# The MLP of a decoder layer: up projection first by block products, then seven rounds of down products

## The reference, cut to what matters

```python
x = x + y                                   # y: the mixer, its last step is merged @ w_out
hm = rms_norm(x, norm_mlp)
x = x + jnp.square(jax.nn.relu(hm @ w_up)) @ w_down      # w_up 1024 x 4096, w_down 4096 x 1024
```

## Time and profile before

| | |
|---|---|
| median of 3 runs | 2209.72 us |
| span of the profiled execution (the page gives no other time of it) | 2207.2 us |
| MLP from its first matmul | 1475.5 to the end, 731.7 us |
| instructions | 33503 |
| HBM read, written | 135.62 MB, 34.89 MB |

### The profile page before, as it was taken

One profiled execution on the slowest core, in us unless ns is written; L12 is line 12 of the kernel. 1 busy time (PEld: TensorE's weight loads), 2 busy tenths in 40 slices (PEclk: granted clock), 3 DMA queues, 4 the chain that ended last, 5 costly groups with the idle time before them and its releaser, 6 DMA issues. The chain is left out here.

```text
span 2207.2 us, 33503 instructions
## 1 busy us (share of the span) xinstructions
PE 2188.0 (99%) x13547; PEld 2073.1 (94%) x13547; DVE 1112.9 (50%) x1749; ACT 658.2 (30%) x1158; POOL 1094.1 (50%) x1363
## 2 busy tenths in 40 slices
PE   8999999999999999999999999999999999999998
PEld 7999999999999999999999999889989889899897
DVE  8522221799764535534443566455364463553625
ACT  5444442333321111232222212133223232232332
POOL 4544444677343233222225564418475575754851
PEclk9999999999999999999999999999999999999999
DMA  5233332112121111222334555201211202102022
GB/s 180 95 99 100 107 104 69 49 49 69 53 89 51 48 42 52 58 60 80 90 121 141 174 186 169 97 16 43 77 30 49 70 8 77 58 20 77 20 67 81
DMA packets 172941, 172.31 MB, mean 78 GB/s; under 512 B 6722, under 2 KB 147334, under 8 KB 172779
## 3 DMA queue, kind: packets, MB, share of 16 engines
q1 hardware_dynamic: 169905, 159.87, 23.6%
q0 software_dynamic: 2304, 8.91, 1.1%
q10 hardware_dynamic: 578, 1.38, 0.2%
HBM read 135.62 MB, written 34.89 MB: 77 GB/s over the span
## 5 line engine op out<-in xcount | busy, mean ns | idle before, releaser
L967 PE MATMUL acc<-h_hi,w_hi 128*128 128x368 f32 (+2 forms) x2040 | 669.6, 328 | 0.5 <-issue 0.5
L969 PE MATMUL acc<-h_hi,w_lo 128*128 128x368 f32 (+2 forms) x2040 | 663.5, 325 | 0.0
L968 PE MATMUL acc<-h_lo,w_hi 128*128 128x368 f32 (+2 forms) x2040 | 662.8, 325 | 0.0
L1952 POOL TENSOR_TENSOR w_lo<-w_raw,w_hi 128x256 fp32r<-128x256 f32 x508 | 378.1, 774 | 470.1 <-ACT w_hi L1464 470.1
L967 PEld LDWEIGHTS acc<-h_hi,w_hi 128*128 128x128 f32 x2040 | 383.4, 188 | 5.5 <-issue 4.0
L968 PEld LDWEIGHTS acc<-h_lo,w_hi 128*128 128x128 f32 x2040 | 383.5, 188 | 0.2
L969 PEld LDWEIGHTS acc<-h_hi,w_lo 128*128 128x128 f32 x2040 | 383.3, 188 | 0.0
L1464 ACT ACTIVATE w_hi<-w_raw 128x1024 fp32r<-128x1024 f32 (+2 forms) x145 | 138.7, 957 | 358.9 <-PE acc L969 183.8
L2310 DVE TENSOR_TENSOR x<-pz,x 128x512 f32<-128x512 f32 x214 | 144.3, 688 | 90.9 <-PE pz L969 88.3
L1952 POOL TENSOR_TENSOR a_op<-a_raw,a_op 128x256 fp32r<-128x256 f32 x196 | 157.8, 843 | 24.6 <-DVE a_raw L2310 14.9
L2310 DVE TENSOR_TENSOR a_raw<-acc,a_raw 128x368 f32<-128x368 f32 (+1 forms) x112 | 44.8, 421 | 206.9 <-ACT a_raw L1827 118.7
(11 more groups left out here) (530 smaller groups left out, 4687.5 us busy)
## 6 DMA issues: line engine op xcount, KB each, us to landing
w_raw<-in_w_in SPq DMA_DIRECT2D x70, 512.0 KB, 4.3
w_raw<-in_w_up SPq DMA_DIRECT2D x32, 512.0 KB, 4.3
gate_values<-staging SPq DMA_DIRECT2D x29, 544.0 KB, 3.7
gsig<-gate_values SPq DMA_DIRECT2D x29, 544.0 KB, 3.7
w_raw<-in_w_down SPq DMA_DIRECT2D x18, 512.0 KB, 3.5
b_raw<-branch_outputs POOLq DMA_DIRECT2D x16, 544.0 KB, 5.5
w_raw<-in_w_branch SPq DMA_DIRECT2D x16, 512.0 KB, 4.8
g_raw<-in_w_in SPq DMA_DIRECT2D x14, 512.0 KB, 5.3
```

What stands on the lines that cost most here:

```text
L967: pe.matmul(out, lh, rh, start=first, stop=False, skip_group_check=more)
L968: pe.matmul(out, lh, rl, start=False, stop=False, skip_group_check=more)
L969: return pe.matmul(out, ll, rh, start=False, stop=last, skip_group_check=more)
L1952: return pool.tensor_tensor(out, x, y, op)
```

## The change

The whole up projection runs before the down projection. Its last four units are computed first and plainly; relu and square are both done by ACT into `staging` and the values are stored to DRAM. The other 28 units go in 14 pairs by seven block products, as at the gates, with sums `t_op` made anew from `h_hi` and `h_lo` by DVE. The residual is stored to DRAM for this (nine DMAs of 512 KB; t_raw takes its place) and is loaded back afterwards into the place of `h_hi`/`h_lo`. DVE adds and squares a pair's values, makes four sums of blocks for the down products, and SP stores these operands: 7 x 256 KB for a pair and 96 KB for the samples. Seven down rounds of seven stages follow without an up part between. u's operands are loaded, 512 KB a stage, into six places; ACT makes the high halves of the weights (`b_high`) and of u (`a_high`), GpSimd the low halves of both. In rounds 2 to 5 the stored values of the last four units are split too (`u_high`, `u_low`), for the end, which is computed as before. Cut to its core:

```diff
-L_UN, L_BN, L_GN, L_IT = 4, 4, 44, 8
+LAST, VP, NR = 4, 14, 7
+OPS_V = 7 * VP
+OPS_D = 7 * NR
+A_SLOTS = 6
+DVE_LO = []
+POOL_LO = [n for n in range(OPS_D) if n not in DVE_LO]
...
 TensorE
-            for i in range(END):
-                for s in range(4):
-                    up(i, s)
-                down(i)
-            for s in range(4):
-                up(END, s)
+            for e in range(LAST):
+                last_up(e)
+            up_pairs()          # as pairs(), weights w_up, 14 pairs
+            for i in range(NR):
+                down(i)
...
 down, TensorE: what a stage waits for
-                        pe.wait_ge(sem("op_lo"), OPS_G + 7 * i + st + 1)
-                        pe.wait_ge(sem("u_ready"), 16 * i + A_READY[st])
+                        pe.wait_ge(sem("op_lo"), OPS_G + OPS_V + n + 1)
+                        pe.wait_ge(*a_low_ready(n))
...
                         if st == 0:
-                            pe.wait_ge(sem("u_ready"), 16 * i + 11)
+                            pe.wait_ge(sem("packed"), i + 1)
...
 ScalarE
+            wide_hi(L_U + 1)
+            for e in range(LAST):
                 for g in range(3):
+                    last_square(e, g)
+                    if (e, g) in ((0, 2), (1, 0), (2, 0), (2, 1)):
+                        v_t_high(((0, 2), (1, 0), (2, 0), (2, 1)).index((e, g)))
+                    if g == 2 and e < 2:
+                        wide_hi(L_U + 2 + e)
...
+            for n in range(2, OPS_D):
+                a_high(n)
+                b_high(n)
+                if n % 7 == 1:
+                    pack_high(n // 7)
+                if n % 7 == 6 and 2 <= n // 7 < 6:
+                    u_high(n // 7 - 2)
...
 GpSimd
+            for e in range(1, LAST):
+                wide_lo(L_U + e)
+            for n in range(OPS_V):
+                v_low(n)
+            b_low(0)
+            a_low(0)
+            a_low(1)
+            for n in range(1, OPS_D):
+                b_low(n)
+                if n + 1 < OPS_D:
+                    a_low(n + 1)
+                if n % 7 == 6 and 2 <= n // 7 < 6:
+                    u_low(n // 7 - 2)
+            e_low(0)
+            e_low(2)
...
+            def a_low(n):
+                pool.wait_ge(hi_ready, L_U + LAST + n + 1)
+                for q in range(2):
+                    for c0 in (0, 256):
+                        c = slice(c0, c0 + 256)
+                        ins = tt(a_lo(n)[:, q, c], a_raw(n)[:, q, c], a_hi(n)[:, q, c].bitcast(F32), ALU.subtract)
+                ins.then_inc(w_ready, 1)
...
 VectorE
+            def v_t_sums():
...
+                dve.wait_ge(sem("b_stored"), 16 * H + 16 * (NT + 1))
+                dve.wait_ge(group_ready, L_G)
+                dve.wait_ge(sem("rows_to_lo"), 4 * (NT + 1))
+                ...                            # nine sums of 128x2176, in a chain
+                v_op_sums(0, (0, 1))
+                for n, t in ((2, 1), (1, 2), (3, 0), (4, 3)):
+                    dve.wait_ge(sem("t_hi"), 4 + n)
+                    tt(t_op[:, t, 1], t_raw[:, t, 1], t_op[:, t, 0].bitcast(F32), ALU.subtract) \
+                        .then_inc(sem("t_lo"), 1)
+                v_op_sums(0, (2,))
...
+            def up_pairs():
+                for j in range(VP):
+                    if j:
+                        v_op_sums(j, (2,))
+                        v_finish(j - 1)        # one square, four sums of 512, two small ones
+                    v_add(j, 1, "11", 0)
+                    v_square(j, "11", "g_dve", 6 * j + 2)
+                    v_op_sums(j, (3,))
+                    if j + 1 < VP:
+                        v_op_sums(j + 1, (0, 1))
+                    v_add(j, 4, "22", 4)
+                    v_square(j, "22", "g_dve", 6 * j + 4)
+                    v_add(j, 5, "21", 2)
+                    v_square(j, "21", "g_dve", 6 * j + 6)
...
+            v_t_sums()
+            up_pairs()
+            down_sums(0, 1)
+            v_finish(VP - 1)
+            dve.wait_ge(sem("g_done"), V_DONE + 2 * OPS_V - 4)
+            link(dve.memset(x1_s[TS:], 0.0))
+            pack_low(0)
...
 SyncE, between the pairs and the rounds
+            sp.wait_ge(sem("g_done"), V_DONE + 2 * OPS_V - 8)
+            op_load(0)
+            op_load(1)
+            sp.wait_ge(sem("op_lo"), OPS_G + OPS_V)
+            f1_load(0)
+            sp.wait_ge(sem("g_done"), V_DONE + 2 * OPS_V - 6)
+            op_load(2)
+            op_load(3)
...
+            for n in range(OPS_D):
+                i, st = n // 7, n % 7
+                if n + A_SLOTS < OPS_D:
+                    sp.wait_ge(group_ready, op_end(n))
+                    op_load(n + A_SLOTS)
+                if st == 3 and i + 1 < NR:
+                    sp.wait_ge(sem("op_sums"), SUMS_D + 8 * i + 8)
+                    sp.wait_ge(sem("op_lo"), OPS_G + OPS_V + 7 * i + 3)
+                    f0_load(i + 1)
+                    sp.wait_ge(sem("op_lo"), OPS_G + OPS_V + 7 * i + 6)
+                    f1_load(i + 1)
```

More of the change, by code:

```diff
@@ L514, in build @@
-        with ExitStack() as st:
[L515 to L522, removed]
+            sb(st, "pad_x", [P, 4832])
+            m_s = sb(st, "m_s", [P, KT, 2 * TS], F32R)
+            spill_o = sb(st, "spill_o", [P, 2, 512])[0:TS]
@@ L1395, in up @@
                         normed_in(g)
                     for k in range(KT):
-                        if first and g == 1 and k == 4:
+                        if e == 0 and g == 1 and k == 4:
                             turn_normed(NT)
-                        cols = slice(k % 4 * P, k % 4 * P + P)
-                        mm = product(acc[:, g, 0:c1 - c0], hi[k // 4][:, cols], lo[k // 4][:, cols],
-                                     h_hi[:, k, c0:c1], h_lo[:, k, c0:c1], k == 0, k == KT - 1)
+                        hi, lo = [w_tile(w, (L_U + e) % SLOTS, k, 0, P) for w in (w_hi, w_lo)]
@@ L1915, in _ @@
+            act.wait_ge(sem("l_added"), 32 * NR)
+            copy(spill_l, x1_s[TS:]).then_inc(sem("spilled"), 1)
             act.wait_ge(sem("folded"), 3)
@@ new lines, in v_t_sums, with made, h @@
+            def v_t_sums():
+                def made(out, x, y, op):
+                    tt(out, x, y, op).then_inc(sem("t_made"), 1)
+                def h(w, k, half):
+                    return w[:, 4 * k:4 * k + 4, half * HT:half * HT + HT].bitcast(F32)
+                dve.wait_ge(sem("b_stored"), 16 * H + 16 * (NT + 1))
+                dve.wait_ge(group_ready, L_G)
+                dve.wait_ge(sem("rows_to_lo"), 4 * (NT + 1))
+                t1, t2, t3, t4 = [t_raw[:, t, 1] for t in range(4)]
+                low = t_raw[:, 3, 0]
+                made(low, h(h_lo, 0, 1), h(h_lo, 1, 1), ALU.subtract)
+                made(t3, h(h_hi, 0, 1), h(h_hi, 1, 1), ALU.subtract)
+                v_t_made(2)
+                made(t3, t3, low, ALU.add)
+                v_t_made(3)
+                made(t2, h(h_hi, 0, 0), t3, ALU.subtract)
+                v_t_made(4)
+                made(t2, t2, h(h_lo, 0, 0), ALU.add)
+                v_t_made(5)
+                made(t1, h(h_hi, 1, 1), t2, ALU.subtract)
+                made(t4, h(h_hi, 1, 0), t2, ALU.subtract)
+                v_t_made(6)
+                made(t1, t1, h(h_lo, 1, 1), ALU.add)
+                v_t_made(7)
+                made(t4, t4, h(h_lo, 1, 0), ALU.add)
+                v_op_sums(0, (0, 1))
[4 more added lines that the diff above has]
+                v_op_sums(0, (2,))
@@ new lines, in v_square, with v_add @@
+            def v_square(j, corner, ready, count):
+                dve.wait_ge(sem(ready), (V_DVE if ready == "g_dve" else V_ACT) + count)
+                v = v_value(j, corner)
+                stt(v, v, 0.0, v, ALU.max, ALU.mult).then_inc(sem("v_squared"), 1)
+            def v_add(j, e, corner, copied):
+                for c in range(2):
+                    dve.wait_ge(sem("g_done"), V_DONE + 14 * j + 2 * e + c + 1)
+                    dve.wait_ge(sem("g_act"), V_ACT + 8 * j + copied + c + 1)
+                    v = v_value(j, corner, c)
+                    tt(v, v_bank(j, e, c), v, ALU.add).then_inc(sem("g_dve"), 1)
```

858 lines of the change are left out of this document (505 added, 353 removed).

## The result

The changed kernel takes 2221.3 us, the median of 4 runs (2220.2 to 2222.5), against 2209.8 beside it: ratio 1.0053, 95% interval 1.0039 to 1.0067. It is slower by 0.5%; I had forecast 2199 and called that side 0.14. The profiled execution has a span of 2218.4 us. First the page, part 1, to be held against the earlier trace rows.

The account below looks back on a forecast made before the run. TensorE, 99% busy, was taken as the bound. Profiled: 2207.2 - 35.8 (pairs) + 8.5 (start) + 2 (clock) + 5 (seam) + 10 (down rounds) = 2196.9 us, so 2199 timed; forecast range 2184 to 2205.

Parts of the forecast that it names:

- Seven down rounds: Rounds without an up part between: GpSimd's work about level with TensorE's 42.38 us a round, costing 10 us.
- rival A: Down rounds: GpSimd is the bound, from 0.757 us a subtraction on; 2230 us, slower than before; chance 0.12.
- Start: Start of the up part: GpSimd's subtractions slowed beside DVE's t_op instructions make TensorE wait, 8.5 us.
- Clock: After the start's wait and the next waits, TensorE runs some matmuls at a lower clock: 2 us.
- Pairs: Fourteen up pairs at 21.17 us each against 23.73 for two plain units save 35.8 us; added waits 0.
- Seam: From the pairs to the down rounds: the samples' product waits for DVE's pack_low(0), 5 us.
- End: End part after the last round: its weights' loads and low halves come in time, cost 0, upper bound 3 us.

Follow-up runs that it names:

- the run with drains: Changed kernel with GpSimd waiting, in the down rounds, after each low half until its last instruction is complete: 2216.7 us, ratio 1.0033.
- e12: Changed kernel with e6's start, e15's low halves on DVE without drains, and the last pair's finish behind stage 0 of the first round: 2181.5 us.
- e15: Changed kernel with the drains, and DVE making the values' low halves of stages 6 and 1 (and 3 in rounds 2 to 5): 2192.6 us.
- e1: Changed kernel without DVE's eight weight sums in each down round; ACT and GpSimd take raw weight blocks instead: 2207.9 us, ratio 0.9991.
- e6: Changed kernel with the up part's start reordered on DVE and ACT, DVE making the low halves of plain units two to four: 2206.9 us.
- e5: Changed kernel with DVE instead of GpSimd making the values' low halves of stages 6 and 1 of the down rounds: 2196.7 us.
- e4: Changed kernel with 14 more GpSimd waits in the down rounds, for DVE's sums of stages 6 and 1: 2215.5 us, ratio 1.0030.
- e8: Changed kernel with DVE making the samples' low half before finishing the last pair, between pairs and rounds: 2223.4 us, ratio 1.0062.
- e10: Changed kernel with one more GpSimd wait per down round, before stage 5's low half, for DVE's stage 6 sums: 2218.4 us.
- e3: Changed kernel with four of five GpSimd instructions left out of each low half of the last values: 2210.5 us, ratio 1.0012.

## Why the prediction was wrong

**Seven down rounds: the step that failed.** I took 10 us; it was 32.9 (23.3 us of waits without the seam's, 9.6 of clock). I had written "So 42.1 to 42.9 us against 42.38, level", with GpSimd as the one that falls behind and "2.9 to 3.7 us a round" for turns. The load was sized fairly: 412 subtractions by my terms are 307 to 312 us, the run with drains shows 316.6, or 0.768 us each against the 0.757 at which I had let rival A begin. Two things were wrong. First, who pays: I took it that the two engines alternate, from rows where they do, and charged 0.46 us a turn to GpSimd. In the rounds GpSimd ran unbroken and single DVE instructions took 5.8 to 7.4 us, and DVE's queue holds the adds that free TensorE's banks. No term of mine had DVE late in the rounds at all, nor did a rival. The instruction of 4.48 us in the trace of before could have warned me. Second, I took level for nearly hidden. Work equal to the cover leaves no room for any turn that goes wrong, and the run with drains shows that with fair turns it isn't even level: 316.6 us of work in 296.7. Fair turns alone give 2216.7 and less load alone 2196.7; with both the rounds lose 6.3 us, 5.2 of them waits and 4.0 of these the seam's. As rounds 1 to 6 of e12 and e15 are alike, the load is the part that has to go; that DVE is kept out decides where the shortage shows. A load just under the cover isn't enough: in e1 GpSimd was busy 289.4 us, and TensorE still waited 13.2 us behind the instruction kept out, the seam aside. Rival A had the load as the cause, too, but not its sign: not all seven rounds took 46 us or more, and no wait in them was named after GpSimd.

The Trainium skill (SBUF - State Buffer, "Who interferes with whom") calls the port pair that the two engines share an exclusive lock, and says that issue order decides who blocks. I read it as one turn, the length of one instruction. The rows show more: the block lasts for 8 to 11 GpSimd instructions in a row in the changed kernel and 13 in e1.

**Start.** The wait after the first unit: 7.4 forecast, 7.50 measured; GpSimd's eight subtractions beside the large sums took 23.08 us, 2.9 each. At the first pair 1.1 forecast, 3.15 measured: the four t_op low halves on DVE are the cause, as I had it, but not by way of GpSimd. I had not followed ACT's queue, where the copies out of PSUM stand behind a high half that waits 6.57 us for a sum which DVE makes behind four t_op low halves (10.51 us). e6 shows both and their price.

**Clock.** 2 us forecast; 2.2 in the plain units (58.07 - 48.4 - 7.5) and 9.6 in the rounds. What I went by (after a wait, some matmuls at 1.2 GHz) holds for some waits; I applied it to the start alone. In e1 a wait of 4.46 us cost some 1.6 us more (eight matmuls 0.43 us apart in place of 0.23).

**Pairs.** 21.17 us forecast; 295.3 / 14 = 21.09 without the wait at the first. The saving against plain units is 37.0, not 35.8: right.

**Seam.** 5 forecast, 4.4 measured, for the packs on DVE, as said. **End.** 54.1 us from its first matmul to the end of the span, 54.0 before, no wait: right.

With these terms, -37.0 + 10.7 + 2.2 + 4.4 + 32.9 = +13.2 us; the MLP took 2218.4 - 1473.85 = 744.5 us from its first matmul, against 731.7 before: +12.8. The rest, 0.4 us, is mostly in the down parts of before, 42.43 us on average and not 42.38.

## What to carry to other kernels

Where two engines share a port, price both of them: write down what stands in the queue of the one that is kept out, for it need not alternate. Compare the work of an engine off the critical path with its cover, turns included, and leave a margin: 316.6 us in 296.7 lost, 283.2 fitted. Its share of busy time doesn't tell: 90% of the rounds in the changed kernel, 91% in e5 and 93% in e15, which lost least. Moving or pausing single instructions moved the loss (e4, e8, e10); taking work off the fuller engine removed most of it. And a wait of TensorE can cost more than its length.

## What the runs showed that I had not expected

A DVE instruction of 0.56 us with two SBUF inputs took 9.15 us beside thirteen GpSimd subtractions in a row; a hole of 0.07 us between two of them is enough to let it in. In the cases of the changed kernel and e1 DVE's instruction ended 0.4 to 0.6 us after GpSimd's run had. What decides, without a hole, between turns (1.2 us) and the long case stays open: in the four traces with the sums and GpSimd's order in the rounds unchanged (the changed kernel, e3, e6, e8) the sums of stage 6 had the long case in all seven rounds and those of stage 3 in none, with the same shapes, and neither the length of GpSimd's run so far nor the moment at which DVE asks told them apart. GpSimd's own subtractions of 128x256 took 0.72 to 0.81 us in the long cases of the changed kernel and e1, so nothing in its rows betrays that it is holding another engine up; only DVE's durations do.
